# Values of eleven token tiles computed inside the attention block instead of at the end of the projection block

## The chip, the cores and the metric

The kernel is one program on one core of a Trainium2 chip. The metric is the device time of one execution in microseconds (us). TensorE is called PE here, VectorE DVE, ScalarE ACT, GpSimd POOL, and SP is the engine that issues the DMAs.

## The reference, cut to what matters

One step of a hybrid decoder layer, for a prompt of 2048 tokens and a sample group of 8 sequences of 8 tokens (64 tokens). All in float32.

```
h = RMSNorm(x)
z = h @ W_in                      # 1024 x 4608, columns shared out to three head groups
y = x + concat[A(h)*silu(g_A), B(h)*silu(g_B), C(h)*silu(g_C)] @ W_out
A: dilated sliding-window attention, 6 heads of 64, three branches merged by their softmax denominators
B: causal convolution and RG-LRU
C: HGRN2, chunkwise gated linear recurrence, 6 heads, key width 128, value width 64
final RMSNorm
```

The change touches `z = h @ W_in` for the columns of A's values (384 columns), and the HGRN2 of the 64 sample tokens.

## The kernel before, in words

There are two blocks, one behind the other, with a barrier between them in which every queue is drained.

**The projection block** (`front`) normalises the input in 17 token tiles (16 of 128 tokens, and one of the 64 sample tokens, tile 16). Each tile is turned on PE and kept as a high and a low part, `f_ht0` and `f_ht1`, of [128, 8, 2112]: eight contraction steps by all tokens. Every product with a weight is done as three matmuls (`mm3`, lines 49 to 51: high by high, high by low, low by high). Where the weights are stationary, the moving operand is a stretch of 384, 448 or 512 tokens; where a token tile is stationary, the moving operand is 384 weight columns. The values (`("t", 2, j)` in the order) are of the second kind: one token tile is 8 steps of 3 matmuls, then an ACT copy (line 665) and a store to the DRAM tensor `zt`. They are the last thing of the block, 17 tiles in a row. Between them stand the last steps of the prompt's HGRN2, which is cut into 30 units (6 heads by 5 token groups) of about 12 "slots" each; `parts()` puts the next slot into the order. Before, one slot stands behind each value tile.

**The attention block** (`attend_project`) is ordered by a list that `attend_schedule` writes. All engines walk the same list, each takes its own part of an entry, and all queues are in order. The entries that matter here:

- `s`, n: quarter n%4 of head n//4's keys (parts 0, 1) or queries (parts 2, 3). A load of 2 x 256 KB from `zf`, an ACT copy to the high part (line 1914), a DVE subtraction for the low part (2104 keys, 2108 queries), and for queries another ACT copy (1918).
- `u`, n: one of 32 units of scores of a head: 2 matmuls on PE (2353, 2354) into one of three banks, mask and minimum on DVE (2118), the exponential on ACT (1966).
- `w`, h: DVE gathers head h's statistics (2030) once its 32 units are done; `x` and `z` exchange them between partitions.
- `t`, `o`, `f`: probabilities are turned by a diagonal matrix that POOL writes (1865, PE 2412), copied on ACT or DVE (1533, 1535), multiplied with the values (2433), stored. They start 11 units behind the scores of their head, so the first is in head 1, behind its eleventh unit.
- `g`, c: the gates' sigmoid in four pieces on ACT (1963), each multiplied on POOL (1850).
- `ha` to `hz`: HGRN2 of the 64 sample tokens: gates and logarithms (1921 to 1937), scan (2140), decays on POOL (1832 to 1841) and ACT (1940 to 1945), pair products `hp` (2333), outputs `ho` (2378, 2380), state updates `hu` (2388 on PE, 2162 and 2165 on DVE), `hq`, `hr`, `hn` the output's norm (1957, 1844, 2174).

Before, the sample's HGRN2 and the gates of the first head pair stand among the 32 units of head 0, which has no `t` and `o` beside it.

Of the kernel before, what the change touches and what calls it, by code (L numbers as in the profile page):

```python
# [9 lines left out]
F32 = mybir.dt.float32  # L10
F32R = mybir.dt.float32r
# [62 lines left out]
def constants(nc, sem, con):  # L74
    made = sem("c_made")
    with nc.Block() as block:
        @block.gpsimd
        def _(pool):
# [5 lines left out]
            pool.wait_ge(made, BASE + 3)  # L84

# [27 lines left out]
def front_schedule():  # L113
# [124 lines left out]
def front(nc, sem, io, con, zf, zt, mab, mt):  # L238
# [7 lines left out]
    with ExitStack() as ctx:  # L246
        def sb(name, shape, dt=F32):
            return ctx.enter_context(nc.sbuf_tensor("f_" + name, shape, dt))

        ht = [sb(f"ht{p}", [P, KD, T], F32R) for p in range(2)]  # L250
        w_raw = sb("wraw", [P, 2 * KD * P])
        w_hi, w_lo = sb("whi", [P, 3072], F32R), sb("wlo", [P, 3072], F32R)
# [28 lines left out]
        sts = sb("sts", [P, 4 * NN + 1])  # L281
# [10 lines left out]
        lbl, tiny = sb("lbl", [P, 4, NH]), sts[:, 4 * NN:]  # L292
# [316 lines left out]
        def _(act):  # L609
# [195 lines left out]
        def _(dve):  # L805
# [11 lines left out]
            def low(i):  # L817
                t0, n = TTILES[i]
                for q in range(2):
                    dve.wait_ge(S["h_hi"], BASE + 2 * i + q + 1)  # L820
                    src = tps[2 * (i % 2) + q][:].rearrange("p (k t) -> p k t", t=P)
                    V.tensor_tensor(ht[1][:, 4 * q:4 * q + 4, t0:t0 + n], src[:, :, :n], ht[0][:, 4 * q:4 * q + 4, t0:t0 + n],
                                    ALU.subtract).then_inc(S["h_lo"], 1)
# [252 lines left out]
        def _(pe):  # L1076
# [24 lines left out]
            def product(s, k0, k1):  # L1101
# [13 lines left out]
            def tile_product(s):  # L1115
# [8 lines left out]
                for k in range(KD):  # L1124
                    if b == 0:
                        pe.wait_ge(S["t_split"], BASE + KD * a + k + 1)
                    mm = mm3(nc, bank[i % 3][:n, :AW], ht[0][:, k, t0:t0 + n], ht[1][:, k, t0:t0 + n],
# [201 lines left out]
ROOM, ROOM_END = 17600, 229376  # L1329


def attend_schedule():

# [12 lines left out]
    for h in range(NH):  # L1346
        for i in range(SB):
# [5 lines left out]
    order, made = [("s", 0), ("s", 1), ("ha", 0), ("s", 2), ("hb", 0)], 0  # L1353
    hgrn = {1: [("hc", 0)], 3: [("s", 3), ("hp", 0)], 5: [("hd", 0)], 8: [("hx", 0)], 10: [("hk", 0), ("he", 0), ("ht", 0)],
            11: [("hp", 1)], 12: [("hz", 0), ("hp", 2)], 13: [("ht", 1)], 14: [("hp", 3), ("ht", 2)], 16: [("ht", 3)],
            24: [("hq", 0)], 27: [("hr", 0)], 28: [("hn", 0)], 31: [("hs", 0)]}
    for h in range(NH):
        hgrn.setdefault(17 + h, []).append(("ho", h))
        hgrn.setdefault((23, 25, 26, 28, 29, 31)[h], []).insert(0, ("hu", h))
# [10 lines left out]
    for u in range(len(units)):  # L1370
        h, k = u // per, u % per
        order.append(("u", u))
        if h == 0:
            order += hgrn.get(k, [])
        if h + 1 < NH and k in (12, 16, 22):
# [7 lines left out]
        if (h, k) in ((0, 26), (1, 26), (3, 28)):  # L1383
            order.append(("g", (0, 1, 3).index(h)))
# [23 lines left out]
def attend_project(nc, sem, io, con, zf, zt, mt, mab):  # L1408
# [21 lines left out]
    with ExitStack() as ctx:  # L1430
# [6 lines left out]
        class Place:  # L1437


            end = ROOM  # L1440

            def __init__(self, words):
                self.at, self.words, self.used = Place.end, words, 0
                Place.end += 4 * words
# [1146 lines left out]
```

## Time and profile before

| | us |
|---|---|
| time, median of 3 runs | 1953.63 (1952.71 to 1958.79) |
| the profiled execution's own time | 1956.31 |
| its span in the trace | 1954.6 |
| PE busy | 1815.5 (93%) |
| DVE busy | 992.7 (51%) |
| ACT busy | 876.7 (45%) |
| POOL busy | 652.5 (33%) |

The busy time of PE is an average over stages. The page's line of 40 slices shows 9 tenths or more nearly everywhere; the slices that fall out are those from about 1150 to 1350 us, where its row of PE's granted clock falls too. Matmuls overlap in the records, so a stretch is read from the distance of the starts.

### The profile page before, as it was taken

Reading aid. Unit: us, or ns where it says so; the run is one execution under the profiler, and the core shown is the slowest. Engines: PE = TensorE matmul, PEld = TensorE weight load, DVE = VectorE, ACT = ScalarE, POOL = GpSimd, SP = SyncE. Lnnn points to the kernel's source line nnn. Section 1 sums busy time; section 2 is a strip of 40 time slices with the busy share of each in tenths; the row PEclk is TensorE's granted clock in tenths of the full one; section 3 lists DMA queues with packets and bytes.
Section 4 is the critical chain, followed back from the end, with each engine's and each line's share of the span. In section 5 each row is a group of like instructions: output and inputs, shape, how many; then the busy total and the mean of one; then the engine's idle time right before and its main releaser. Section 6 shows DMA issues by size and latency. Waiting matters only on the chain. (4 is left out here: it accounts for less than half of the span.)

```text
span 1954.6 us, 29631 instructions
## 1 busy us (share of the span) xinstructions
PE 1815.5 (93%) x10840; PEld 1583.7 (81%) x10840; DVE 992.7 (51%) x2034; ACT 876.7 (45%) x1650; POOL 652.5 (33%) x882
## 2 busy tenths in 40 slices
PE   6999988999999999999999995778989998999998
PEld 6978878898999899999989894557777886666665
DVE  4437644224666666666666523554545456454542
ACT  4438762114555655565555512655666431111110
POOL 1103212003565556556555411144333432112110
PEclk9999999999999999999999997779999999999999
DMA  6311111132021211102110115552341074665641
GB/s 201 94 43 34 38 57 48 58 112 71 24 58 27 56 29 47 36 23 60 28 56 25 36 51 118 132 104 72 103 103 33 25 226 148 184 211 170 184 144 50
DMA packets 181769, 162.12 MB, mean 83 GB/s; under 512 B 65433, under 2 KB 168890, under 8 KB 180858
## 3 DMA queue, kind: packets, MB, share of 16 engines
q1 hardware_dynamic: 181626, 160.24, 29.1%
q8 instruction: 87, 1.43, 0.3%
q14 instruction: 56, 0.46, 0.1%
HBM read 116.89 MB, written 46.55 MB: 84 GB/s over the span
## 5 line engine op out<-in xcount | busy, mean ns | idle before, releaser
L49 PE MATMUL f_bank<-f_ht,f_whi 128*128 128x384 f32 (+2 forms) x1080 | 403.5, 374 | 5.7 <-DVE f_wlo L831 5.7
L50 PE MATMUL f_bank<-f_ht,f_whi 128*128 128x384 f32 (+2 forms) x1080 | 383.1, 355 | 0.0
L51 PE MATMUL f_bank<-f_ht,f_wlo 128*128 128x384 f32 (+2 forms) x1080 | 382.9, 355 | 0.0
L780 ACT ACTIVATE f_scr<-f_scr 128x384 f32<-128x384 f32 (+1 forms) x210 | 114.5, 546 | 270.6 <-POOL f_scr L562 270.3
L49 PEld LDWEIGHTS f_bank<-f_ht,f_whi 128*128 128x128 f32 x1080 | 204.9, 190 | 19.9 <-DVE f_wlo L831 6.5
L50 PEld LDWEIGHTS f_bank<-f_ht,f_whi 128*128 128x128 f32 x1080 | 204.9, 190 | 13.4 <-issue 1.7
L51 PEld LDWEIGHTS f_bank<-f_ht,f_wlo 128*128 128x128 f32 x1080 | 204.2, 189 | 13.1
L1142 PE MATMUL f_tps<-f_scr 128*128 128x128 f32 x1536 | 204.6, 277 | 2.3 <-DVE f_scr L975 2.3
L1142 PEld LDWEIGHTS f_tps<-f_scr 128*128 128x128 f32 x1536 | 193.9, 192 | 5.1 <-DVE f_scr L975 2.5
L975 DVE TENSOR_TENSOR f_scr<-f_scr 128x192 f32<-128x192 f32 (+1 forms) x210 | 100.9, 481 | 180.1 <-ACT f_scr L780 179.9
L1865 POOL TENSOR_SCALAR a_diag<-c_ident,a_wt 128x128 f32<-128x128 f32 x192 | 119.3, 641 | 129.3 <-DVE a_wt L2187 97.6
L561 POOL TENSOR_TENSOR f_scr<-f_scr 128x192 f32<-128x192 f32 (+1 forms) x210 | 134.3, 639 | 82.8 <-PE f_tps L1142 80.5
L966 DVE COPY_PREDICATED f_scr<-f_scr,f_tps 128x384 f32<-128x384 int32 (+1 forms) x210 | 130.4, 621 | 44.7 <-PE f_tps L1142 35.9
L49 PE MATMUL f_bank<-f_whi,f_ht 128*128 128x384 f32 (+1 forms) x408 | 142.2, 349 | 3.1 <-DVE f_wlo L835 3.1
L50 PE MATMUL f_bank<-f_wlo,f_ht 128*128 128x384 f32 (+1 forms) x408 | 137.9, 338 | 0.0
L51 PE MATMUL f_bank<-f_whi,f_ht 128*128 128x384 f32 (+1 forms) x408 | 137.6, 337 | 0.0
L49 PE MATMUL a_s<-a_whi,a_mhi 128*128 128x512 f32 (+1 forms) x306 | 123.6, 404 | 4.7 <-DVE a_y L2283 4.7
L50 PE MATMUL a_s<-a_wlo,a_mhi 128*128 128x512 f32 (+1 forms) x306 | 120.3, 393 | 0.0
L587 POOL TENSOR_SCALAR f_scr<-f_scr,f_lbl 128x384 f32<-128x384 f32 (+1 forms) x30 | 46.0, 1534 | 211.3 <-ACT f_scr L747 211.3
L1884 POOL TENSOR_TENSOR a_small<-a_small,c_mhalf 128x1 f32<-128x1 f32 (+1 forms) x17 | 9.4, 551 | 280.8 <-DVE a_small L2287 280.8
L2433 PE MATMUL a_o<-a_pt,a_vf 128*64 128x128 f32 x480 | 68.1, 285 | 17.2 <-ACT a_pt L1533 16.2
L49 PEld LDWEIGHTS f_bank<-f_whi,f_ht 128*128 128x128 f32 (+1 forms) x408 | 76.5, 188 | 6.5 <-DVE f_wlo L835 4.9
(381 smaller groups left out, 3616.3 us busy)
## 6 DMA issues: line engine op xcount, KB each, us to landing
f_wraw<-in_w_in SPq DMA_DIRECT2D x27, 512.0 KB, 4.1
a_raw<-zf SPq DMA_DIRECT2D x48, 256.0 KB, 4.3
zt<-f_stage SPq DMA_DIRECT2D x48, 192.0 KB, 1.9
a_k<-in_ck SPq DMA_DIRECT2D x48, 192.0 KB, 3.8
a_v<-in_cv SPq DMA_DIRECT2D x48, 192.0 KB
f_scr<-in_xp SPq DMA_DIRECT2D x16, 512.0 KB, 4.6
a_x<-in_xp SPq DMA_DIRECT2D x16, 512.0 KB, 4.8
out_y_prompt<-a_y SPq DMA_DIRECT2D x16, 512.0 KB, 2.9
```

What stands on the lines that cost most here:

```text
L49: nc.tensor.matmul(out, w_hi, m_hi, start=start, stop=False)
L50: nc.tensor.matmul(out, w_hi, m_lo, start=False, stop=False)
L51: return nc.tensor.matmul(out, w_lo, m_hi, start=False, stop=stop)
L561: G.tensor_tensor(d[:, :, hs:], b[:, :, hs:], r, ALU.subtract)
L587: G.tensor_scalar(key[:, :n], key[:, :n], lbl[:, 1, h:h + 1], None, ALU.mult).then_inc(S["gated"], 1)
L780: A(lev[i % 3][:, :n], lev[i % 3][:, :n], ACT.Exp).then_inc(S["expd"], 1)
L966: V.copy_predicated(attn[:, :n].rearrange("p (j t) -> p j t", t=P), m.bitcast(I32).unsqueeze(1).to_broadcast([P, nt, P]), lp[x % 2][:, :n] ...
L975: V.tensor_tensor(e[:, :, hs:], e[:, :, hs:], q[:, :, hs:], ALU.mult).then_inc(S["xlev"], 1)
L1142: mm = nc.tensor.matmul(lp[x % 2][:, cols], left[:, cols], right[:, cols], start=True, stop=True)
L1865: G.tensor_scalar(diag[:, 2 * NC * (b % 2) + NC * far + m, :], con["ident"][:], wt[h % 2][:, far, c:c + 1], None, ALU.mult).then_inc(S["di ...
L1884: G.tensor_tensor(s[:, 2:3], s[:, 1:2], con["mhalf"][:rows_of(n), 0:1], ALU.pow).then_inc(Z["rstd"], 1)
L2433: mm = nc.tensor.matmul(out, val, pt[n % 4][:, c * P:(c + 1) * P], start=first and c == 0, stop=n in ends and c == len(blocks) - 1)
```

## The change

In the projection block the normed input is laid out tile by tile: `c_ht` is [128, 13, 2, 8, 128] (token tile, high or low, contraction step, token), and the last 448 tokens are in `c_htail` of [128, 2, 8, 448]. A moving operand of 384 or 512 tokens in the first thirteen tiles is now 3 or 4 pieces of 128 tokens. Only the first six value tiles (`J0 = 6`) stay, each with two slots of HGRN2 behind it instead of one. Both tensors and the split weights have fixed addresses now, so that they stay in place over the barrier, and the attention block's buffers lie over each other and over them in another way.

In the attention block eleven value tiles follow as 22 halves of 12 matmuls (`va`, `vb`), 7 before the first unit of scores and 15 among head 0's units, one behind every second unit; `vb` has an ACT copy to a stage buffer, and the next `va` entry on SP stores it. Waits `tile_out` and `probs_free` keep a buffer from being written before the tile under it has been used. Of the loads ahead of the first unit, the two parts of the gate's and query's sample columns go first, and the queries' raw quarters (`raw2`, `raw3`) only once value tile 7 is done. The load of the values for A (`load_v(0)`) comes at the end of head 0. The sample's HGRN2 is spread otherwise: its lower bound comes from the projection block, `h_qdb` is two small buffers that are cleared, its value blocks `h_vb` are made by POOL (`hv`) instead of ACT, the state updates `hu` and the first gates `g` stand among head 1's units, and the gates' sigmoids have four buffers.

```diff
+J0 = 6
+HT13, HTAIL, TW, FREE = 0, 13 * 2 * D, 13 * 2 * D + 2 * KD * 448, 13 * 2 * D + 2 * KD * 448 + 6 * D
+def normed(con, p, k, t0, n):
+    if t0 >= FG[-1][0]:
+        t0 -= FG[-1][0]
+        return con["htail"][:, p, k, t0:t0 + n]
+    j = t0 // P
+    return con["ht"][:, j, p, k, :] if n <= P else con["ht"][:, j:j + n // P, p, k, :]
...
-    for j in range(XTILES):
+    for j in range(J0):
         add(("t", 2, j))
         parts()
+        parts()
...
-                             ht[0][:, k, t0:t0 + n], ht[1][:, k, t0:t0 + n], k == 0, k == KD - 1)
+                             normed(con, 0, k, t0, n), normed(con, 1, k, t0, n), k == 0, k == KD - 1)
...
+    halves = [(h, j) for j in range(J0, XTILES) for h in ("va", "vb")]
+    for step in ("ha", "va", "vb", "s0", "hb", "va", "hp", "s1", "ht", "hc", "vb", "s2", "hd", "va", "vb", "hx", "s3", "va"):
...
+    later = {2: [("hu", 0)], 3: [("hu", 1), ("hv", 2)], 5: [("hu", 2), ("hv", 3)], 6: [("hu", 3), ("g", 0), ("hv", 4)],
+             7: [("hu", 4), ("hv", 5)], 9: [("hu", 5)], 10: [("hs", 0)]}
...
+        if h == 0 and k % 2:
+            order += hgrn.get(k // 2, [])
+            if halves:
+                order.append(halves.pop(0))
...
+            def store_v(j):
+                t0, n = TTILES[j]
+                sp.wait_ge(VS["out"], BASE + j - J0 + 1)
+                sp.dma_start(zt[t0:t0 + n, TV:TV + AW], stage[j % 2][:n, :]).then_inc(v_store[j % 2], 16)
...
+                elif kind == "vb" and n == J0 + 1:
+                    tile_out(sp, n)
+                    load_raw(2)
+                    load_raw(3)
...
-            for t, v in ((h_cut, 1.0), (h_tiny, 1.0e-37), (h_attn, 0.0), (h_qdb, 0.0)):
+            for t, v in ((h_cut, 1.0), (h_attn, 0.0), (h_qdb[0], 0.0), (h_qdb[1], 0.0)):
...
+                elif kind == "hv":
+                    if n >= 2:
+                        pool.wait_ge(H["us"], BASE + n - 1)
+                    G.tensor_tensor(h_vb[n % 2][:], h_vv[:, hv(n)].unsqueeze(1).to_broadcast([NS, NB, HD]),
+                                    h_rowm[:].unsqueeze(2).to_broadcast([NS, NB, HD]), ALU.mult).then_inc(H["vb_r"], 1)
...
+                elif kind == "vb":
+                    j, rows = n, TTILES[n][1]
+                    act.wait_ge(VS["sum"], BASE + j - J0 + 1)
+                    if j >= J0 + 2:
+                        act.wait_ge(v_store[j % 2], BASE + 16 * ((j - J0) // 2))
+                    A(stage[j % 2][:rows, :], v_bank[j % 2][:rows, 0:AW], ACT.Copy).then_inc(VS["out"], 1)
...
                 elif kind == "hu":
-                    if n == 0:
-                        pe.wait_ge(H["kd_copied"], BASE + 1)
-                        pe.wait_ge(H["vb_r"], BASE + NB)
+                    pe.wait_ge(H["vb_r"], BASE + n + 1)
+                    pe.wait_ge(H["kd_copied"], BASE + 2)
...
+                elif kind in ("va", "vb"):
+                    t0, rows = TTILES[n]
+                    if kind == "va" and n >= J0 + 2:
+                        pe.wait_ge(VS["out"], BASE + n - J0 - 1)
+                    for k in range(KD // 2) if kind == "va" else range(KD // 2, KD):
+                        cols = slice(k * AW, (k + 1) * AW)
+                        mm = mm3(nc, v_bank[n % 2][:rows, 0:AW], normed(con, 0, k, t0, rows), normed(con, 1, k, t0, rows),
+                                 con["whi"][:, cols], con["wlo"][:, cols], k == 0, k == KD - 1)
```

On PE, head 0's first units of scores before (names: `a_khi`, `a_klo` are the keys' high and low parts, `a_qst` the queries, `a_h_` the sample's HGRN2):

```order
L2357 MATMUL a_x<-c_ident,a_h_lrow 128x6
L2353 MATMUL a_s<-a_khi_14220,a_qst 128x128
L2354 MATMUL a_s<-a_klo_14222,a_qst 128x128
L2353 MATMUL a_s<-a_khi_14220,a_qst 128x128
L2354 MATMUL a_s<-a_klo_14222,a_qst 128x128
```

The same engine among head 0's units in the changed kernel, at the end of one half tile and the beginning of the next:

```order
L50 MATMUL a_o<-c_wlo,c_ht 128x384
L51 MATMUL a_o<-c_whi,c_ht 128x384
L2442 MATMUL a_s<-a_khi_13904,a_qst 128x128
L2443 MATMUL a_s<-a_klo_13906,a_qst 128x128
L2442 MATMUL a_s<-a_khi_13904,a_qst 128x128
L2443 MATMUL a_s<-a_klo_13906,a_qst 128x128
L2422 MATMUL a_t<-a_h_lev_13983 64x64 x6
L49 MATMUL a_o<-c_whi,c_ht 128x384
```

Between two pairs of units there are now twelve matmuls of the values; before, the first four units stood directly behind one another.

On PE in head 1, ahead of the first turned probabilities (`a_diag`), in the changed kernel:

```order
L2474 MATMUL a_t<-a_h_vb_13987,a_h_kdt 128x512
L2442 MATMUL a_s<-a_khi_13905,a_qn 128x256
L2443 MATMUL a_s<-a_klo_13907,a_qn 128x256
L2474 MATMUL a_t<-a_h_vb_13986,a_h_kdt 128x512
L2442 MATMUL a_s<-a_khi_13905,a_qst 128x256
```

The state updates (2474) stood among head 0's units before. On POOL the value blocks of two of them stand behind the four multiplications of the first gates:

```order
L1946 TENSOR_TENSOR a_gs_13933<-a_gs_13933,a_gsig_13955 128x512
L1946 TENSOR_TENSOR a_gs_13933<-a_gs_13933,a_gsig_13956 128x512
L1946 TENSOR_TENSOR a_gs_13933<-a_gs_13933,a_gsig_13957 128x512
L1946 TENSOR_TENSOR a_gs_13933<-a_gs_13933,a_gsig_13958 128x512
L1936 TENSOR_TENSOR a_h_vb_13986<-a_h_vv,a_h_rowm 64x512
L1936 TENSOR_TENSOR a_h_vb_13987<-a_h_vv,a_h_rowm 64x512
L1961 TENSOR_SCALAR a_diag<-c_ident,a_wt_13950 128x128 x24
```

So the fifth update waits for POOL behind the gates.

## Rows read from the trace of the kernel before

**Rows 1.** Busy us of the engines in stretches of 50 us, PE's granted clock, DMA

```profile
1150.00:1200.00 50.00, 44.18 (x262) 42.92 (x260) 2.09 (x7) 5.62 (x12) 2.13 (x6) 0.97 0.13 44
1200.00:1250.00 50.00, 21.74 (x117) 17.96 (x118) 30.77 (x88) 30.25 (x66) 13.22 (x24) 0.53 0.90 181
1250.00:1300.00 50.00, 35.58 (x192) 23.89 (x191) 25.31 (x83) 30.63 (x77) 14.02 (x19) 0.68 0.35 85
```

**Rows 2.** Timeline of ACT, copies of value tiles 5, 8, 15, 16 (start, us, idle before)

```profile
1145.72 0.49 ACT L665 ACTIVATE f_stage<-f_bank 128x384 f32<-128x384 f32 x1 [3.96 <-PE f_bank L51]
...
1160.94 0.49 ACT L665 ACTIVATE f_stage<-f_bank 128x384 f32<-128x384 f32 x1 [5.01 <-PE f_bank L51]
...
1190.06 0.49 ACT L665 ACTIVATE f_stage<-f_bank 128x384 f32<-128x384 f32 x1 [3.67 <-PE f_bank L51]
1194.22 0.48 ACT L665 ACTIVATE f_stage<-f_bank 64x384 f32<-64x384 f32 x1 [3.67 <-PE f_bank L51]
```

**Rows 3.** Timeline of DVE, the last instruction of the prompt's HGRN2

```profile
1163.60 0.36 DVE L1020 TENSOR_TENSOR f_scr<-f_scr 128x192 f32<-128x192 f32 x1
```

**Rows 4.** Timeline of POOL, start of the attention block

```profile
1198.72 0.14 POOL L1803 IOTA a_pcol<- 128x1 int32 x1 [35.55 <-POOLq L1655]
...
1200.38 2.65 POOL L1808 MEMSET a_h_qdb<- 128x3072 f32 x1
```

**Rows 5.** Timeline of DVE, the masks and the first keys' low parts

```profile
1200.66 2.52 DVE L2020 TENSOR_SCALAR a_pn<-a_pn,a_pcf 128x256 int32<-128x256 int32 x1
...
1204.38 0.43 DVE L1277 TENSOR_SCALAR a_pn<-a_pn 128x512 int32<-128x512 int32 x1
...
1210.01 2.29 DVE L2104 TENSOR_TENSOR a_klo<-a_raw,a_khi 128x1024 fp32r<-128x1024 f32 x2
```

**Rows 6.** Timeline of ACT, first query part, first exponential, a later query part, decays

```profile
1213.86 1.06 ACT L1918 ACTIVATE a_qn<-a_qst 128x1024 fp32r<-128x1024 f32 x1 [2.44 <-DVE a_qst L2108]
...
1218.57 0.40 ACT L1966 ACTIVATE a_pf<-a_pf,a_sf 128x128 f32<-128x128 f32 x1 [2.13 <-DVE a_sf L2118]
...
1225.66 1.04 ACT L1914 ACTIVATE a_qst<-a_raw 128x1024 fp32r<-128x1024 f32 x1
1228.21 1.06 ACT L1918 ACTIVATE a_qn<-a_qst 128x1024 fp32r<-128x1024 f32 x1 [1.51 <-DVE a_qst L2108]
...
1232.35 1.33 ACT L1945 ACTIVATE a_h_lev<-a_h_lev 128x384 f32<-128x384 f32 x3
```

**Rows 7.** DMA issues from 1194 to 1300 us (count, KB each, median us to landing)

```profile
a_raw<-zf SPq DMA_DIRECT2D x20, 256.0 KB, 4.4
```

**Rows 8.** Timeline of PE, a unit of scores and an output of HGRN2 (full clock)

```profile
1251.95 0.32 PE L2378 MATMUL a_x<-a_h_vv,a_h_attn 64*64 64x64 f32 x2
...
1253.28 0.39 PE L2353 MATMUL a_s<-a_khi,a_qn 128*128 128x256 f32 x1
1253.51 0.28 PE L2354 MATMUL a_s<-a_klo,a_qn 128*128 128x256 f32 x1
1253.72 0.33 PE L2378 MATMUL a_x<-a_h_vv,a_h_attn 64*64 64x64 f32 x2
```

**Rows 9.** Timeline of DVE, one state update, and the stall at the norm

```profile
1266.79 0.69 DVE L2162 TENSOR_TENSOR a_h_s<-a_h_s,a_h_gl 128x512 f32<-128x512 f32 x1
1267.52 0.69 DVE L2165 TENSOR_TENSOR a_h_s<-a_h_s,a_o 128x512 f32<-128x512 f32 x1
...
1280.28 0.55 DVE L2174 TENSOR_TENSOR a_h_oc<-a_x,a_h_small 64x384 f32<-64x384 f32 x1 [7.86 <-POOL a_h_small L1844]
```

**Rows 10.** Timeline of ACT, the first gates, and the first copy of turned probabilities

```profile
1269.68 1.28 ACT L1963 ACT_TABLE_LOAD   x1
1270.97 0.63 ACT L1963 ACTIVATE a_gsig<-a_gs 128x512 f32<-128x512 f32 x1
...
1277.63 1.28 ACT L1966 ACT_TABLE_LOAD   x1
...
1296.25 0.60 ACT L1533 ACTIVATE a_pt<-a_t 128x512 f32<-128x512 f32 x1 [0.29 <-PE a_t L2412]
```

**Rows 11.** Timeline of POOL, the first gate multiplication

```profile
1271.68 1.26 POOL L1850 TENSOR_TENSOR a_gs<-a_gs,a_gsig 128x512 f32<-128x512 f32 x1 [41.38 <-ACT a_gsig L1963]
```

**Rows 12.** Timeline of DVE, head 0's statistics

```profile
1285.18 0.29 DVE L2030 TENSOR_TENSOR a_exch<-a_sf,a_quarter 128x128 f32<-128x128 f32 x1
```

**Rows 13.** Groups by form from 1500 to 1600 us (busy us, mean ns)

```profile
L2354 PE MATMUL a_s<-a_klo,a_qn 128*128 128x256 f32 x16 | 4.3, 282 | 0.0
...
L2354 PE MATMUL a_s<-a_klo,a_qst 128*128 128x256 f32 x4 | 1.1, 279 | 0.0
```

More of the change, by code:

```diff
@@ L1328 @@
 KM = 3 * AW // P
-ROOM, ROOM_END = 17600, 229376
 def attend_schedule():
@@ L1372, in attend_schedule @@
         order.append(("u", u))
-        if h == 0:
-            order += hgrn.get(k, [])
-        if h + 1 < NH and k in (12, 16, 22):
+        if h == 0 and k % 2:
+            order += hgrn.get(k // 2, [])
+            if halves:
+                order.append(halves.pop(0))
+            if k + 1 == per:
+                assert not halves
+                order.append(("ve", 0))
+        if h == 1:
+            order += later.get(k, [])
+        if h and h + 1 < NH and k in (12, 16, 22):
             order.append(("s", 4 * (h + 1) + (12, 16, 22).index(k)))
@@ L1535, in evacuate @@
                 nc.vector.tensor_copy(pt[t % 4][:, :w], tp[t % 2][:, :w]).then_inc(S["copied_v"], 1)
-        raw += [vals0.again().tile(f"raw{p}", [P, SEQ // 2]) for p in (2,)] + [vals0.tile("raw3", [P, SEQ // 2])]
+        raw3 = Place(done0 + 2 * D, 2 * D)
+        raw += [raw3.tile(f"raw{p}", [P, SEQ // 2]) for p in (2, 3)]
+        ints_at = Place(FREE + 6144, 2048).tile("ints", [P, SEQ])
+        gsig0 = [turned.again().tile(f"gsig0{r}", [P, CLS]) if r == 0 else turned.tile(f"gsig0{r}", [P, CLS]) for r in range(NC)]
@@ L1551, in attend_project @@
[L1551 to L1553 removed]
+        stage = [early.tile(f"stage{r}", [P, AW]) for r in range(2)]
+        h_kk, h_qc, h_kd, h_bb, h_lk, h_qd, h_cut, h_sq = (early.tile("h_" + n, [P, W]) for n in ("kk", "qc", "kd", "bb", "lk", "qd", "cut", "sq"))
@@ new lines, in attend_project @@
+        h_rowm = late.tile("h_rowm", [NS, NB])
+        lev_at = late.used
+        h_lev = [late.tile(f"h_lev{l}", [P, W]) for l in LV]
+        late.used = lev_at
+        h_vb = [late.tile(f"h_vb{p}", [NS, NB, HD]) for p in range(2)]
+        h_lbl, h_tiny, h_op = con["lbl"], con["tiny"], bank_x
+        v_bank = [bank_o[:, b * 512:(b + 1) * 512] for b in range(2)]
+        VS = {x: sem("v_" + x) for x in ("sum", "out")}
+        v_store = [sem(f"v_store{r}") for r in range(2)]
+        NV = XTILES - J0
@@ L1563, in attend_project, with tile_out, probs_free, bank_h @@
         hw = lambda h: slice(h * P, (h + 1) * P)
+        def tile_out(eng, j):
+            eng.wait_ge(VS["sum"], BASE + j - J0 + 1)
+        def probs_free(eng, u):
+            h, i, far, m = units[u]
+            if h == 0:
+                j = NC * i + m
+                tile_out(eng, J0 + ((0, 0, 4, 1)[i] if far else 0 if j < 2 else 2 if j < 10 else 3))
+            elif h == 1:
+                tile_out(eng, XTILES - 1)
+        ring_h = [("P", 0), ("K", 0), ("K", 1)] + [("P", n) for n in (1, 2, 3)] + [("U", h) for h in range(NH)]
+        def bank_h(kind, n):
+            return bank_t[ring_h.index((kind, n)) % 2]
+        def bank_h_free(eng, kind, n):
+            e = ring_h.index((kind, n))
+            if e >= 2:
+                kind, n = ring_h[e - 2]
+                eng.wait_ge(H[{"P": "taken", "K": "kd_copied", "U": "s_new"}[kind]], BASE + n + 1)
         def hgrn_over(eng):
```

270 lines of the change are left out of this document (142 added, 128 removed).

## The prediction

> **What bounds the kernel now.** I read the busy shares first, then the table of stretches, then the timelines of each engine from the last value tiles to the first turned probabilities. PE is busy 93% of the span, so what is worth looking for is the place where it is not. The table of stretches [rows 1] shows it: from 1150 to 1200 us PE is busy 44 of 50 us at a granted clock of 0.97 (the level of 2.4 GHz), from 1200 to 1250 only 21.7 of 50 at 0.53 (mostly the level of 1.2 GHz), and from 1250 to 1300 35.6 at 0.68. In those 100 us no engine is full: DVE has 56 us, ACT 61. They are the start of the attention block and head 0's scores, where chains from engine to engine set the pace. Just ahead PE does nothing but the values, one tile every 4.16 us (1194.22 - 1190.06, [rows 2]), that is 24 matmuls of 0.173 us from start to start. The change takes eleven of these tiles from the full stretch into the loose one. In the following, B is the start of the attention block, POOL's first instruction at 1198.72 [rows 4].
>
> **The projection block.** From the copy of value tile 5 to that of tile 16 there are 1194.22 - 1145.72 = 48.5 us [rows 2], and 11 tiles of 4.16 are 45.8; the other 2.7 us are work of HGRN2's last slots on PE, which the change puts ahead of tile 5. So the block ends 45.8 us earlier if PE stays full: **-45.8**. The drain, store and barrier behind it stay as they are.
>
> The slots are two per tile now. Before, HGRN2 ended at 1163.96 [rows 3], behind ten slots with a tile each, while the new block would end on PE at about 1194.2 - 45.8 = 1148.4. The last unit's chain goes in turn through POOL, ACT, DVE and PE for each of its levels, and in the double slot behind tile 1 PE waits for ACT's copy of the turned decays with no tile in between, where before it had one. Lower bound 0 (PE had no gap there before, and the order is otherwise the same), upper bound 15.6, when the chain ends no earlier than before. One double slot costs two or three round trips of about 1 us that a tile hid; I take **+3**.
>
> The new layout changes how a moving operand is read: 3 or 4 pieces of 128 tokens instead of one. The nearest rows are scores at the full clock from 1500 to 1600 us [rows 13]: near keys, 256 columns in 8 pieces of 32, take 282 ns, far keys, 256 in one piece, 279. So at most 3 ns for each of the some 2,600 such matmuls, 8 us; since these have fewer pieces, I take **0**. The copies on ACT and DVE that write the layout have as many elements as before.
>
> **The attention block up to head 0's end.** Before, this takes from B to head 0's statistics at 1285.18 [rows 12], 86.5 us. Now:
>
> - PE starts tiles 6 and 7 at once. It then waits for the sample's pair product, which needs the gated key from DVE. DVE does its masks first, until B+11.3 (1210.01, [rows 5]). One of them, 256 elements, took 2.52 us beside POOL's memset of `h_qdb` (2.65 us, [rows 4]), while a mask of 512 took 0.43 [rows 5]. The memset is now two of 576 elements instead of 3072, so I count the masks 1 us shorter. Then 1.15 us for the keys' low part, 1.1 us for key and query, about 1.5 for the pair product, 2.1 for the second half of tile 7: B+16.
> - Only then are the queries' raw quarters loaded, 4.4 us to landing [rows 7]: B+20.5. Before, they had been there by B+11. The query part takes 1.04 us, the DVE subtraction, 1.06: 3.6 us from 1225.66 to 1229.27 [rows 6]: B+24. The decays with their table load (1.28 + 2.3) and the copy of tile 8 stand next on ACT, then the second query part with another 3.6 us: ACT is at the first exponential at B+31.5. Before it was there at B+19.9 (1218.57, [rows 6]). So the prelude is **11.6 us longer**; tiles 8 and half of 9 fit into it, 6.2 us.
> - Then PE has 32 units and 15 halves. A half is 12 x 0.173 = 2.08 us. A single unit of 256 columns takes 1253.72 - 1253.28 = 0.44, an output of HGRN2 1253.28 - 1251.95 = 1.33 [rows 8]. Two units in a row come to about 0.6 us at 128 or 256 columns (12 pairs), 0.8 and 1.05 at 384 and 512 (2 each): 10.9. HGRN2 adds 6 x 1.33 = 8 for outputs and about 5.4 for pair products and turns. With 0.15 for each entry into a half: 31.2 + 10.9 + 8 + 5.4 + 2.2 = 57.7, of which 4.2 have been done by B+30.4. ACT has about 34 us in the same time and DVE 30, so PE leads, and waits of the three score banks fall into the halves. 53.5 us of PE from B+30.4 is B+84; for a stretch at the lower clock at the start I add 1.5 to 3 us, for the last exponential 1.5. **Head 0's statistics at B+87**, against 86.5 before: +0.5. Bounds: B+79 (clock full, entries free) to B+97.
>
> **From head 0's end to the first turned probabilities.** Before this takes 1296.25 - 1285.18 = 11.1 us [rows 10, 12]. Now there are six state updates and the first gates in it. An update is 0.69 + 0.69 us on DVE [rows 9], 8.3 us for six; four stand ahead of the gates, of which some 4.5 us aren't covered. The gates: ACT loads a table twice, 1.28 us each, and does 4 x 0.63 [rows 10], 5.1 us; the four buffers spare it the alternation with POOL, which made it 9.2 us before (1269.68 to 1278.91). But POOL multiplies four times at 1.26 [rows 11], from 1.9 us behind the start, and the fifth update's value block stands behind these on POOL: 1.9 + 5 + 1.3 = 8.3 us until PE may go on with it, and behind that update PE has the units 40 to 42. Then the last two updates and units, about 4 us. 8.7 + 4.5 + 8.3 + 5.5 = 27 us: **+16**. Before, a stall of the same kind stood in head 0, DVE 7.86 us [rows 9]; it is in the 86.5. Lower bound +4 (all updates covered, gates as ACT alone), upper +20.
>
> The values for A are loaded at head 0's end, 2 MB; in the trace this took about 12 us, and they are needed 27 us later. Cover enough; if it were gone, the wait would be on PE's first `o`. Everything behind stands in the same order, and I count it the same.
>
> **Sum.** -45.8 + 3 + 0 + 0.5 + 16 = -26.3. The profiled execution took 1956.3 us with a span of 1954.6; this is 2.7 above the median of the runs. 1953.6 - 26.3 = 1927.3: **1927 us**.
>
> **Rivals.**
>
> - *The moved work is hidden altogether*: the stalls of updates and gates fall into time that before was lost too, the prelude's extra 11.6 us are made good as the halves keep the clock at the upper level. For it: 42.7 us of 100 were idle on PE in [rows 1] at a clock near 0.6. Against it: the gates' wait is on an in-order queue. -45.8 + 3 = 1911 us. Chance 0.2.
> - *The tail of HGRN2 sets the end of the projection block*: chain as long as before, +15.6 instead of 3: 1940 us. For it: one slot per tile was all that hid it. Against: the chain had waits of 4 to 10 us for PE's tiles in it. Chance 0.13.
> - *The clock stays at the lower level in the block.* Halves take 4.16 us instead of 2.08, 15 in the loop, +31 us, less the 3 counted: 1955 us, no change. For it: the granted clock was 0.53 and 0.68 in [rows 1]. [...] Chance 0.07. The Trainium skill ("TensorE: Matmul & The Clock Gate", the section on the second HAM failure mode, psum-queue depth-cycling) says that short idle times between groups of matmuls can make the clock go back and forth; [rows 1] agree that a PE with gaps gets less, and that would be this rival.
> - *Slower: the pieces of the moving operand cost time at each matmul.* It would be all over the projection block, from the first weights on. It decides from 26.3 us / 2,600 = 10 ns per matmul; at twice that, +52: 1979 us. For it: no row shows pieces 8 KB apart. Against: 3 ns in [rows 13] with more pieces. Chance 0.05.
>
> The Trainium skill ("GPSIMD Engine Reference", key points) says that GpSimd shares its SBUF interfaces with VectorE and that the two contend; the 2.52 us against 0.43 in [rows 5] agree. It stands here only for the 1 us of the masks.
>
> **How the numbers follow.** The forecast has 0.55, with its own range 1918 to 1937. Below 1908 it would take more than the whole of the moved tiles. 8 in 10 reach from the hidden case to the tail's: 1909 to 1943. Under 0.3% (5.9 us) a measurement of this kernel can't be told from no change: the clock's rival is that, in part. Faster 0.92, same 0.04, slower 0.04.
>
> **What the profile after would show.** Right: the attention block starts near 1156 (1198.7 - 42.8); value matmuls in the projection of the same 0.173 us; the first exponential 31 us behind B; PE busy over 40 of 50 us in head 0 at a clock above 0.9; statistics of head 0 at B+87; POOL's value block behind the gates with PE waiting some 3 us beyond ACT's table load; first turned probabilities at B+114. Wrong: PE gaps of over 5 us among the last six value tiles, half tiles of 4 us, or 10 ns more per matmul before 1100 us.

## The result and the profile after

The changed kernel takes 1934.2 us (median of 4 runs, 1931.0 to 1936.6) against 1955.8 (4 runs, 1952.7 to 1958.8). The ratio is 0.989 with a 95% interval of 0.986 to 0.992. A second set of 4 runs gave 1934.2 (1932.5 to 1934.7) and 0.989 (0.988 to 0.991). The forecast was 1927. By the medians the change is worth 21.6 us, where the sum said 26.3. The span of the profiled execution is 1930.1 us against 1954.6, -24.5; a second profile of the changed kernel, from the second set, has 1932.5. One of the eleven runs of the experiment e2 below took 2648.9 us at a mean granted clock of 0.64 and is left out of its figures.

Three marks split both spans: B (GpSimd's first instruction in the attention block), head 0's statistics (DVE's `a_exch<-a_sf`), and ACT's first copy of turned probabilities.

| us | start to B | B to statistics | statistics to first copy | first copy to end |
|---|---|---|---|---|
| before [rows 4, 10, 12] | 1198.7 | 86.5 | 11.1 | 658.4 |
| after | 1152.9 | 89.4 | 29.2 | 658.6 |
| after, second profile | 1158.2 | 86.5 | 28.9 | 658.8 |
| difference, first profile | -45.8 | +2.9 | +18.1 | +0.2 |
| forecast | -42.8 | +0.5 | +16 | 0 |

The table of stretches of after, with the columns of [rows 1]:

```profile
1150.00:1200.00 50.00, 37.65 (x200) 35.98 (x201) 19.72 (x50) 23.35 (x47) 13.01 (x28) 0.80 0.49 131
1200.00:1250.00 50.00, 47.76 (x326) 40.28 (x324) 24.12 (x87) 23.73 (x71) 4.42 (x4) 0.95 0.34 95
1250.00:1300.00 50.00, 37.36 (x209) 28.24 (x208) 24.68 (x65) 29.20 (x66) 22.32 (x31) 0.78 0.71 166
```

The stretch of head 0's scores is now full: PE 47.8 of 50 us at 0.95, where [rows 1] have 21.7 at 0.53. The loose place has moved on to 1250, head 1's start.

**The projection block.** One event ahead of the moved work dates the traces: ACT's last copy of a product with stationary weights, 8 us ahead of the copy of the first value tile. The first fence is from before; the second, from after, has the copy of the last value tile too:

```profile
1108.24 0.52 ACT L680 ACTIVATE f_stage<-f_bank 128x448 f32<-128x448 f32 x1
```

```profile
1105.22 0.52 ACT L700 ACTIVATE f_stage<-f_bank 128x448 f32<-128x448 f32 x1
...
1148.72 0.49 ACT L685 ACTIVATE f_stage<-f_bank 128x384 f32<-128x384 f32 x1 [3.45 <-PE f_bank L51]
```

So 3.0 us of the -45.8 had arisen by there, ahead of all moved work. From 250 to 300 and from 300 to 350 us the granted clock was 0.92 and 0.94 in the one execution and 0.93 and 0.97 in the other, and from 100 to 150 us 0.93 and 0.97. This differs from execution to execution: in the second profile of the changed kernel the same copy comes at 1110.49, 2.3 us later than before. From this event to B it is 90.48 us before and 47.70 after: **-42.8**, which is what the forecast had (-45.8 + 3). The second profile has 47.74. The +3 is idle time of PE among the double slots (start, us, in brackets the idle time before):

```profile
1115.39 0.43 PE L1177 MATMUL f_op<-f_scr 128*128 128x64 f32 x2 [0.82 <-DVE f_scr L986]
1124.12 0.55 PE L1247 MATMUL f_tps<-c_ident,f_scr 128*128 128x128 f32 x3 [0.28 <-ACT f_scr L804]
1125.98 0.88 PE L1256 MATMUL f_tps<-f_scr 128*128 128x64 f32 x6 [1.31 <-ACT f_scr L816]
1138.73 0.43 PE L1177 MATMUL f_op<-f_scr 128*128 128x64 f32 x2 [0.82 <-DVE f_scr L986]
```

That is 3.2 us in all, where the kernel before had one gap of 0.28. The third row is the round trip to ACT that the forecast named. From the dated event to the last value copy PE is busy 45.4 us less than before and idle 3.0 us more.

**From B to head 0's statistics.** B itself, the mask that [rows 5] had at 2.52 us, the memset beside it, and DVE's first low part, all of after:

```profile
1152.92 0.14 POOL L1890 IOTA a_pcol<- 128x1 int32 x1 [6.14 <-POOLq L1729]
...
1154.56 1.09 POOL L1895 MEMSET a_h_qdb<- 128x576 f32 x2
```

```profile
1154.86 0.93 DVE L2117 TENSOR_SCALAR a_ints<-a_ints,a_pcf 128x256 int32<-128x256 int32 x1
...
1162.63 1.16 DVE L2201 TENSOR_TENSOR a_klo<-a_raw,a_khi 128x1024 fp32r<-128x1024 f32 x1
```

The masks were 1.6 us shorter (1 was counted), the low part at B+9.7 (forecast B+10.3). Then PE's wait for the pair product, ACT's for the raw queries, and the first exponential:

```profile
1164.77 1.54 PE L2422 MATMUL a_t<-a_h_qc,a_h_kk 128*64 128x64 f32 x12 [3.90 <-DVE a_h_qc L2223]
```

```profile
1174.83 1.06 ACT L2012 ACTIVATE a_qst<-a_raw 128x1024 fp32r<-128x1024 f32 x1 [4.11 <-DMA a_raw<-zf]
...
1185.30 0.39 ACT L2062 ACTIVATE a_pf<-a_pf,a_sf 128x128 f32<-128x128 f32 x1
```

The exponential is at B+32.4 (forecast 31.5). The two parts of head 0 in the table of stretches, and the statistics:

```profile
1152.92:1185.30 32.38, 24.62 (x116) 23.59 (x117) 16.15 (x35) 17.66 (x27) 11.97 (x27) 0.76 0.62 161
1185.30:1242.34 57.04, 53.56 (x379) 49.42 (x378) 21.19 (x79) 26.86 (x80) 3.38 (x3) 0.96 0.26 77
```

```profile
1242.34 0.29 DVE L2127 TENSOR_TENSOR a_exch<-a_sf,a_quarter 128x128 f32<-128x128 f32 x1 [1.79 <-ACT a_pnb L2062]
```

PE is busy 53.6 of 57.0 us in the loop, so it leads there, as forecast. Statistics at B+89.4 (forecast 87). The second profile has the same two stretches:

```profile
1158.23:1189.96 31.73, 25.31 (x122) 24.33 (x122) 16.17 (x35) 17.46 (x27) 11.95 (x27) 0.80 0.63 164
1189.96:1244.74 54.78, 50.55 (x374) 46.47 (x373) 21.01 (x78) 26.55 (x80) 3.38 (x3) 1.00 0.28 81
```

**From there to the first copy.** The stretch before (first fence) and after (second):

```profile
1285.18:1296.25 11.07, 7.31 (x44) 6.61 (x45) 6.85 (x35) 7.33 (x26) 3.93 (x7) 0.50 0.92 197
```

```profile
1242.34:1271.55 29.21, 19.17 (x56) 9.36 (x57) 15.72 (x47) 12.63 (x32) 16.50 (x21) 0.54 0.56 121
```

PE works 11.9 us more and idles 6.3 us more (10.0 against 3.8); together 18.1. Nearly all the idle time is one row, and GpSimd's rows say why:

```profile
1244.77 2.03 PE L2474 MATMUL a_t<-a_h_vb,a_h_kdt 64*128 64x512 f32 x2
...
1263.10 2.07 PE L2474 MATMUL a_t<-a_h_vb,a_h_kdt 64*128 64x512 f32 x2 [9.26 <-POOL a_h_vb L1936]
```

```profile
1257.12 4.93 POOL L1946 TENSOR_TENSOR a_gs<-a_gs,a_gsig 128x512 f32<-128x512 f32 x4 [9.21 <-ACT a_gsig L2059]
1262.01 2.04 POOL L1936 TENSOR_TENSOR a_h_vb<-a_h_vv,a_h_rowm 64x512 f32<-64x512 f32 x2
```

```profile
1255.12 1.28 ACT L2059 ACT_TABLE_LOAD   x1
...
1271.55 0.60 ACT L1574 ACTIVATE a_pt<-a_t 128x512 f32<-128x512 f32 x1 [1.21 <-PE a_t L2511]
```

GpSimd stood 9.21 us in front of the gates' multiplications with the fifth value block behind them, and PE stood in front of that block. Each update also costs PE 2.0 us at the clock of 0.54.

### The profile page after: what moved, and what is told of

Its sections match the earlier page's. It is cut to its first block and busy times, and to the rows that moved or that the text cites. A ratio compares the mean times of both kernels' runs of the same rounds, so it can differ in the third digit from the quotient of the medians.

```text
span 1930.1 us, 29621 instructions
## 1 busy us (share of the span) xinstructions
PE 1811.6 (94%) x10839; PEld 1581.4 (82%) x10839; DVE 990.5 (51%) x2026; ACT 870.6 (45%) x1641; POOL 653.9 (34%) x888
## 5 line engine op out<-in xcount | busy, mean ns | idle before, releaser
L49 PE MATMUL f_bank<-c_ht,c_whi 128*128 128x384 f32 (+1 forms) x864 | 318.8, 369 | 5.7 <-DVE c_wlo L851 5.7
L50 PE MATMUL f_bank<-c_ht,c_whi 128*128 128x384 f32 (+1 forms) x864 | 303.5, 351 | 0.0
L51 PE MATMUL f_bank<-c_ht,c_wlo 128*128 128x384 f32 (+1 forms) x864 | 303.3, 351 | 0.0
L49 PEld LDWEIGHTS f_bank<-c_ht,c_whi 128*128 128x128 f32 x864 | 163.5, 189 | 16.1 <-DVE c_wlo L851 6.5
L50 PEld LDWEIGHTS f_bank<-c_ht,c_whi 128*128 128x128 f32 x864 | 163.4, 189 | 9.7 <-issue 1.1
L51 PEld LDWEIGHTS f_bank<-c_ht,c_wlo 128*128 128x128 f32 x864 | 163.1, 189 | 9.4
L1961 POOL TENSOR_SCALAR a_diag<-c_ident,a_wt 128x128 f32<-128x128 f32 x192 | 118.0, 635 | 120.4 <-DVE a_wt L2277 86.5
L607 POOL TENSOR_SCALAR f_scr<-f_scr,c_lbl 128x384 f32<-128x384 f32 (+1 forms) x30 | 46.0, 1534 | 211.3 <-ACT f_scr L767 211.3
L49 PE MATMUL f_bank<-c_whi,c_ht 128*128 128x384 f32 x256 | 90.8, 355 | 3.2 <-DVE c_wlo L855 3.2
L50 PE MATMUL f_bank<-c_wlo,c_ht 128*128 128x384 f32 x256 | 87.1, 340 | 0.0
L51 PE MATMUL f_bank<-c_whi,c_ht 128*128 128x384 f32 x256 | 87.0, 340 | 0.0
L2062 ACT ACTIVATE a_pf<-a_pf,a_sf 128x128 f32<-128x128 f32 (+3 forms) x96 | 53.5, 557 | 72.2 <-DVE a_sf L2216 71.9
```

The lines of the kernel that those rows point to most:

```text
L49: nc.tensor.matmul(out, w_hi, m_hi, start=start, stop=False)
L50: nc.tensor.matmul(out, w_hi, m_lo, start=False, stop=False)
L51: return nc.tensor.matmul(out, w_lo, m_hi, start=False, stop=stop)
L1961: G.tensor_scalar(diag[:, 2 * NC * (b % 2) + NC * far + m, :], con["ident"][:], wt[h % 2][:, far, c:c + 1], None, ALU.mult).then_inc(S["di ...
L2062: A(probs(n), probs(n), ACT.Exp, bias=stat(n, 0), scale=-1.0, accum_out=stat(n, 1)).then_inc(S["exped"], 1)
```

## The experiments

All times are medians; the changed kernel has 1934.2. Its eight runs spread from 1931.0 to 1936.6, so a difference of 5 us between medians is no larger than this spread, and is read together with the marks in the traces. "Distance" is that from head 0's statistics to the first copy.

**e1, GpSimd's value blocks ahead of the gates.**

```
-    6: [("hu", 3), ("g", 0), ("hv", 4)], 7: [("hu", 4), ("hv", 5)]
+    6: [("hu", 3), ("hv", 4), ("hv", 5), ("g", 0)], 7: [("hu", 4)]
```

> Edit to the changed kernel: GpSimd's last two value blocks of HGRN2 (for the updates of heads 4 and 5) are placed ahead of the first gates instead of behind and between them; nothing else. In the changed kernel PE waited 9.26 us for such a block, and the first copy of turned probabilities came 29.2 us after head 0's statistics. Theory (the forecast's reason for its +16: GpSimd's in-order queue holds PE): PE's wait in front of the fifth update falls below 3 us, the distance becomes 24 to 26 us, and the whole kernel is 3 to 5 us shorter than the changed one, 1927 to 1931 us. Rival (ACT's gates and table loads set the pace there whatever the order): the wait only moves to another row, the distance stays at 28 us or more and the time is the same. Against the kernel before: ratio 0.987 by the theory, 0.989 by the rival.

1929.2 us (1928.6 to 1931.3), ratio 0.987 (0.985 to 0.988). The wait of 9.26 is gone and one of 4.14 for the diagonals stands in its place; the distance is 1267.28 - 1242.60 = 24.7 us:

```profile
1258.15 2.07 PE L2474 MATMUL a_t<-a_h_vb,a_h_kdt 64*128 64x512 f32 x2
...
1265.09 1.65 PE L2511 MATMUL a_t<-a_diag,a_pna 128*128 128x128 f32 x6 [4.14 <-POOL a_diag L1961]
```

The theory holds: the order on GpSimd cost 4.5 us of the distance (4.3 against the second profile's 28.9).

**e2, the layout alone, on the kernel before.**

```
-        ht = [sb(f"ht{p}", [P, KD, T], F32R) for p in range(2)]
+        htm, htt = sb("htm", [P, 13, 2, KD, P], F32R), sb("htt", [P, 2, KD, 448], F32R)
```

(and every use of `ht` through `normed`.)

> Edit to the kernel before: the normed input is laid out tile by tile, as the change has it (thirteen token tiles with high part, low part and eight chunks of 128 columns each, and a tail of 448 tokens); nothing is moved. About 2,600 matmuls of the projection read it as moving or stationary operand, the wide ones now in 3 or 4 pieces of 128 columns that lie 8 KB apart. Theory (the forecast's 0): matmuls of 384 columns go on starting every 0.173 us, the ratio to the kernel before is within 0.997 to 1.003. Rival (the pieces cost time at each matmul, from 10 ns on as the forecast put it): 26 us or more, ratio 1.013 or higher.

1955.8 against 1955.5 us, ratio 1.001 (1.000 to 1.002). Groups by form from 500 to 1100 us, of before and then of this run (busy us, mean ns). 384 columns lie in three pieces in the new layout, 512 in four:

```profile
L50 PE MATMUL f_bank<-f_ht,f_whi 128*128 128x384 f32 x388 | 130.7, 337 | 0.0
L51 PE MATMUL f_bank<-f_ht,f_wlo 128*128 128x512 f32 x120 | 47.2, 393 | 0.0
```

```profile
L50 PE MATMUL f_bank<-f_htm,f_whi 128*128 128x384 f32 x388 | 130.6, 337 | 0.0
L51 PE MATMUL f_bank<-f_htm,f_wlo 128*128 128x512 f32 x120 | 47.1, 393 | 0.0
```

To the nanosecond the same. The pieces cost nothing that these rows show, and the rival of 10 ns is out.

**e3, value tile 7 directly behind tile 6.**

```
-  "ha", "va", "vb", "s0", "hb", "va", "hp", "s1", "ht", "hc", "vb", "s2", "hd", "va", "vb", "hx", "s3", "va"
+  "ha", "va", "vb", "s0", "va", "vb", "hb", "hp", "s1", "ht", "hc", "va", "s2", "hd", "vb", "hx", "s3", "va"
```

> Edit to the changed kernel: in the prelude the two halves of value tile 7 stand directly behind those of tile 6, ahead of the sample's key, pair product and first copy; the load of the queries' raw quarters waits for tile 7 and is issued that much earlier. Theory (the forecast's step: the late load makes the prelude 11.6 us longer): the load is issued 5 to 8 us earlier, the first exponential comes at 25 to 28 us from the start of the attention block instead of 32.4, head 0's statistics at 83 to 86 instead of 89.4, and the time is 3 to 6 us less than the changed kernel's. Rival (PE has the same sum of work up to head 0's end, and the clock is at its lower level in this stretch, so only idle time of PE can be won): statistics at 87.5 or later, 0 to 2 us.

1929.2 us (1927.6 to 1930.2), ratio 0.986 (0.985 to 0.988). The load of the queries' quarters is issued 11.4 us behind B instead of 17.3, and ACT no longer waits for it (B is 1157.61 here):

```profile
1174.49 1.04 ACT L2012 ACTIVATE a_qst<-a_raw 128x1024 fp32r<-128x1024 f32 x1
...
1185.27 0.38 ACT L2062 ACTIVATE a_pf<-a_pf,a_sf 128x128 f32<-128x128 f32 x1
```

First exponential B+27.7, statistics B+83.8: in the theory's windows, and the kernel is 5.0 us shorter. One reserve: in the second profile of the changed kernel, where B fell at 1158.23, the exponential came at B+31.7 and the statistics at B+86.5, not 89.4. Against this profile with nearly the same B the edit is worth 4.1 us at the exponential and 2.7 at the statistics. From B to the end it is 770.8 us, against 774.3 in that profile and 777.2 in the first.

**e4, the fifteen half tiles of head 0's loop in one piece ahead of it.**

```
-    for step in (..., "hx", "s3", "va"):
+    for step in (..., "hx", "s3", "va") + ("va",) * 15:
```

> Edit to the changed kernel: the fifteen half tiles that stand between head 0's units are placed in one piece ahead of the first unit, so that the values still are in the attention block but not among the scores; the rest keeps its order. This measures what the overlap is worth. Theory: PE has 15 x 2.08 = 31.2 us there in which no unit runs, and head 0's loop then takes what it took before without them: head 0's exponentials of the kernel before took 66.6 us with updates and gates in them, of which the 18 that the first stretch of head 1 now takes are gone; so statistics of head 0 at about 32 + 31 + 48 = 111 us from the start of the block, 22 more than the changed kernel, and about 1955 us, no gain over the kernel before. Rival (the loop is bound by PE whatever stands in it): it takes 57.7 - 31.2 = 26.5 us without the halves, the order of the halves makes no difference, statistics at 89 to 92 and 1932 to 1936 us.

1944.8 us (1942.0 to 1947.6), ratio 0.995 (0.993 to 0.996); statistics at B+99.9. Neither number was met: it is between the two. From B to the first exponential and from there to the statistics:

```profile
1155.06:1215.55 60.49, 53.67 (x285) 51.69 (x286) 15.46 (x31) 21.63 (x35) 11.97 (x27) 0.89 0.43 121
1215.55:1254.94 39.39, 27.73 (x211) 22.43 (x209) 21.57 (x82) 23.04 (x71) 3.38 (x3) 0.81 0.21 61
```

Without halves in it the loop takes 39.4 us, PE busy for 27.7 at a clock of 0.81. With them it takes 57.0, PE busy for 53.6 at 0.96. So 31.2 us of matmuls cost 17.6 among the units (15.4 against the second profile's 54.8): the interleaving hides 13.6 us (15.8). Of these the prelude gives back about 3 (60.5 against 32.4 + 31.2), which leaves the 10.5 by which the statistics come later and the kernel is longer.

**e6, the projection's last tiles in halves, a slot behind each.**

```
     for j in range(J0):
-        add(("t", 2, j))
-        parts()
-        parts()
+        add(("E", 2, j))
+        parts()
+        add(("t", 2, j))
+        parts()
```

(`E` is PE's first four of the eight chunks; `t` is the other four and everything else of the tile.)

> Edit to the changed kernel, in the projection block alone: each of the six last value tiles is issued on PE in two halves with one slot of HGRN2 behind each, instead of the whole tile and then two slots. PE had gaps of 0.82, 0.28, 1.31 and 0.82 us in these double slots, 3.2 in all, where the kernel before had 0.28. Theory (the forecast's +3 is what a round trip costs when no tile stands between two slots): the gaps fall below 1 us together, the attention block starts 2 to 3 us earlier at 1150 to 1151, and the time is that much less than the changed kernel's. Rival (the last unit's chain through POOL, ACT, DVE and PE sets the end): the gaps turn up in other places and the start stays within 0.5 us of 1152.9.

1929.2 us (1924.7 to 1931.1), ratio 0.986 (0.985 to 0.988). The four gaps are gone without others in their place. B is 1149.48, 3.4 us earlier than in the changed kernel, but this execution was already 2.6 us behind that one at the event that dates the traces (1107.83 against 1105.22):

```profile
1107.83 0.52 ACT L701 ACTIVATE f_stage<-f_bank 128x448 f32<-128x448 f32 x1
...
1145.28 0.49 ACT L686 ACTIVATE f_stage<-f_bank 128x384 f32<-128x384 f32 x1 [3.67 <-PE f_bank L51]
```

From there to the last value copy it is 37.45 us against 43.50, so the edit is worth 6.0 us, twice what the theory said; the run e8 below has 37.45 too. PE is idle for 3.8 us less (1.4 against 5.1), and for the same matmuls it is busy for 2.3 us less, at a clock of 0.95 instead of 0.92. So the term of +3 is shown as what it was said to be, round trips inside double slots and not the end of a chain, but taking them away gave back some clock as well. The kernel gained 5.0 us by the medians.

**e7, ACT's sigmoids early, GpSimd's multiplications in pairs.**

```
-    later = {2: [("hu", 0)], 3: ..., 5: [("hu", 2), ("hv", 3)], 6: [("hu", 3), ("g", 0), ("hv", 4)], 7: [("hu", 4), ("hv", 5)], ...
+    later = {2: [("gs", 0), ("hu", 0)], 3: ..., 5: [("hu", 2), ("hv", 3), ("ga", 0)],
+             6: [("hu", 3), ("hv", 4), ("gb", 0), ("hv", 5)], 7: [("hu", 4)], ...
```

> Edit to the changed kernel: the value blocks of the last two updates stand as in the run e1_value_blocks_first or at most two gate multiplications later, ACT's sigmoids of the first gates stand ahead of head 1's first update (four buffers hold them, their input landed by 1243.4 in the changed kernel's trace), and GpSimd's four multiplications stand in two pairs in the places where it waited for PE. With the value blocks first, PE's last wait was 4.14 us for the diagonals, which GpSimd made behind the multiplications, and the first copy of turned probabilities came 24.7 us after head 0's statistics. Theory (what is left of the +16 is GpSimd's queue: value blocks, multiplications, diagonals in a row): the diagonals begin 5 to 7 us earlier, PE's wait for them falls below 1 us, the copy comes 19 to 22 us after the statistics, and the kernel is 7 to 9 us shorter than the changed one. Rival (ACT's table loads and sigmoids, 4.8 us, now stand in front of head 1's first exponentials and PE then waits for score banks or updates instead): distance 24 us or more, no gain over e1_value_blocks_first.

1929.1 us (1925.2 to 1929.8), ratio 0.986 (0.985 to 0.988), distance 24.3: no gain over e1, as the rival had it. The theory's first steps held, the diagonals began 14.4 us behind the statistics, where e1 had 20.7, and PE's wait for them is 0.33; but ACT's copy of a raw quarter now stood behind the table loads, DVE waited for that, and PE for DVE's state:

```profile
1247.50 1.28 ACT L2059 ACT_TABLE_LOAD   x1
...
1253.09 1.04 ACT L2012 ACTIVATE a_qst<-a_raw 128x1024 fp32r<-128x1024 f32 x1
```

```profile
1254.16 2.39 DVE L2205 TENSOR_TENSOR a_qst<-a_raw,a_qst 64x1024 fp32r<-64x1024 f32 x1 [3.70 <-ACT a_qst L2012]
```

```profile
1258.87 2.04 PE L2474 MATMUL a_t<-a_h_vb,a_h_kdt 64*128 64x512 f32 x2 [3.97 <-DVE a_h_s L2257]
...
1265.12 1.62 PE L2511 MATMUL a_t<-a_diag,a_pna 128*128 128x128 f32 x6 [0.33 <-POOL a_diag L1961]
```

**e8, the edits of e3, e6 and e7 together.**

> The changed kernel with three edits at once: the last value tiles of the projection in halves with a slot behind each (3.4 us earlier start of the attention block when alone), value tile 7 directly behind tile 6 in the prelude (head 0's statistics 5.6 us nearer to the start of the block when alone), and the gates as in the run e7_sigmoids_early. Theory (three separate stretches, each on the path that sets the end): the gains add up, 3.4 + 5.6 + 7 to 9 = 16 to 18 us less than the changed kernel, span behind the start of the attention block 762 to 765 us against 777.2, time 1915 to 1919 us. Rival (they share one cover, so that what one saves the next waits for): 1922 to 1927 us.

**1917.6 us** (1915.7 to 1919.3), ratio 0.981 (0.979 to 0.982): 16.6 us under the changed kernel, and better than both kernels. The single edits had 5.0, 5.0 and 5.1 us, so within the spread of the runs they add up. B is 1148.80, statistics B+85.2, distance 24.2, rest 657.8. The time was in the theory's window, but by two errors that cancel: the tail is worth 6.0 us where 3.4 were counted (from the dated event to B it is 41.7 us), and behind B it takes 767.1 us, above the theory's 762 to 765, since the gates gave 5.0 instead of 7 to 9 and head 0 4.3 instead of 5.6 (1.4 against the second profile of the changed kernel).

**e9, e8 with the last query part ahead of the sigmoids; e10, e8 with the sigmoids three units later.**

```
e9:  -    2: [("gs", 0), ("hu", 0)]        +    2: [("s", 7), ("gs", 0), ("hu", 0)]     (s 7 left out at unit 4)
e10: -    2: [("gs", 0), ("hu", 0)]        +    2: [("hu", 0)]
     -    5: [("hu", 2), ...]              +    5: [("gs", 0), ("hu", 2), ...]
```

> The kernel of e8_three_together with one step moved: the low part of head 1's last query quarters (the step s 7: ACT's copy of the raw quarter, DVE's subtraction, ACT's second copy) stands ahead of the early sigmoids instead of behind them. In that kernel DVE waited 4.06 us for this copy behind ACT's table loads and sigmoids, and PE 4.31 us for DVE's state behind it. Theory (the early sigmoids gained nothing because they moved the wait from GpSimd's queue to ACT's): both waits fall below 1 us, the first copy of turned probabilities comes 20 to 22 us after head 0's statistics instead of 24.2, and the time is 2 to 4 us less than of e8_three_together, 1913.5 to 1915.5 us. Rival (behind these waits is the sum of PE's own work at its lower clock, six updates of 2.07 us and the units, or a wait of DVE for the same chain): 0 to 1 us, 1916.5 to 1918.5 us.

> The kernel of e8_three_together with the early sigmoids moved three units later, behind the last query part of head 1 and ahead of the third update; the multiplications stay in their two pairs. Theory (what counts is that no copy that DVE waits for stands behind the sigmoids): ACT is at the table load about 13 us behind head 0's statistics, the sigmoids are done 4.8 us later, GpSimd's last multiplication some 2 us behind that and the diagonals start there; PE's wait for DVE goes, one of 1 to 3 us for a value block or the diagonals comes, distance 22 to 24 us, 1916 to 1918 us. Rival (order on ACT is free there): as e9_last_part_ahead, 1913.5 to 1915.5 us.

e9: 1917.6 us (1914.9 to 1919.0), ratio 0.980 (0.978 to 0.981). e10: 1919.6 us (1918.0 to 1921.1), 0.981 (0.979 to 0.983). The kernel before had 1958.3 us in the runs beside these two and 1955.5 beside e8, and the intervals of all three ratios overlap, so differences of 2 us among e8, e9 and e10 are not shown by the times; the distances tell more. In e9 PE's wait for DVE has gone from 4.31 in e8 to 2.21 us, and yet the distance is 24.2:

```profile
1242.63 2.04 PE L2479 MATMUL a_t<-a_h_vb,a_h_kdt 64*128 64x512 f32 x2 [2.21 <-DVE a_h_s L2262]
```

```profile
1233.73:1257.90 24.17, 19.93 (x56) 9.59 (x57) 18.75 (x47) 12.41 (x32) 15.82 (x17) 0.53 0.63 145
```

PE is busy 19.9 of 24.2 us at 0.53, DVE 18.75; in e8 PE was busy 19.1 of 24.2 at 0.55. What is left is mainly PE's own work at the lower level of its clock. The rival of e9 held. In e10 neither side did: PE waited 5.89 us for a value block, more than the theory's 1 to 3, and its distance is 26.7, where the theory had 22 to 24. The order on ACT is not free.

```profile
1252.18 2.07 PE L2479 MATMUL a_t<-a_h_vb,a_h_kdt 64*128 64x512 f32 x2 [5.89 <-POOL a_h_vb L1941]
```

## Why the prediction was right

- **-45.8 for eleven tiles, +3 for the tail.** -42.8 and -42.7 in the two profiles from the dated event on, against -42.8; PE's busy time fell by 45.4 us and its idle time rose by 3.0. The double slots cost 3.2 us of PE, and e6 took them away. What the forecast did not see is that with these gaps closed the clock rises too, so that e6 gained 6.0. That B itself moved by 45.8 is luck: in the second profile of the changed kernel B was 1158.23, with a clock of 0.90 and 0.93 from 250 to 350 us. More than half of that came back: its statistics were at B+86.5, the end 2.4 us later in place of 5.3.
- **0 for the layout.** Shown by e2: 337 and 337 ns, 393 and 393.
- **+0.5 up to head 0's statistics.** +2.9 and +0.0 in the two profiles. The late raw load was the right reason for the long prelude (first exponential B+32.4 and B+31.7, forecast 31.5), shown by e3 (B+27.7 with the load 5.9 us earlier). What differs between the two profiles is the loop: 57.0 us at a clock of 0.96 against 54.8 at 1.00, where the forecast's 53.5 us of PE were counted at the full clock.
- **+16 for the updates and gates in head 1.** +18.1 and +17.9. The mechanism was right: GpSimd's in-order queue put the fifth value block behind the gates. From ACT's table load to the update it took 8.0 us, against 8.3; PE's wait was 9.26, as it stood there 1.3 us ahead of the table load. e1 took 4.5 us of the distance away. The size came out with some luck: of the four terms of 27, 8.7 stands on no row, and for the last updates and units the text says about 4 and the sum takes 5.5. One term was off by its reason: an update was priced by DVE's two instructions [rows 9], 1.4 us, while PE's own matmul for it is 2.0 us at the lower clock; the six are 12 of the 19.2 us that PE is busy there. In e1 and e9 19 to 20 of the 24 to 25 us are PE's own work, so that order alone had only some 5 us left to win.
- **0 behind the first copy.** 658.4 and 658.6 us; 657.8 to 659.5 in all the experiments.
- **The time.** 1934.2 is 6.9 us above the 1927.3 of the sum: 4.7 because the change was worth 21.6 us and not 26.3, and 2.2 because the kernel before has a median of 1955.8 by four runs and the forecast started from 1953.6. From the dated event to the end the two profiles have 21.5 and 24.4 us less than before. So the 24.5 by the first spans, close to 26.3, has 3.0 us in it that had arisen ahead of the change.

Of the rivals, *hidden altogether* would have needed head 1's start to be as short as before. *The tail* had its round trips but no chain behind them. *The clock at its lower level* was true of the prelude, in part (0.76), but the loop had 0.96: half tiles fill PE's gaps, and the clock rose as they did. The Trainium skill ("TensorE: Matmul & The Clock Gate", the section on the second HAM failure mode, psum-queue depth-cycling) speaks of gaps that make the clock go back and forth; e4 agrees from the other side, the same units without the halves having 0.81. *Slower by the pieces* fell with e2.

## What to carry to other kernels

Work of the engine that bounds one stage, moved into a stage where that engine idles, gains its full time where it came from and pays only in part where it lands (here 31.2 us of matmuls for 17.6), if it is cut into pieces that stand among the waits. One length of piece was tried, 2.08 us; how the gain depends on it is not shown. What it wins where it came from is only half of the account: of the 42.8 us won here, 21 were paid back behind in the one profile and 18 in the other, 18 of them for the updates and gates that had to make room. What it pushes out must be priced on every engine that takes part, the matrix engine at its lower clock included, and followed through each in-order queue it joins: a short instruction behind another engine's long chain costs the wait of the whole chain. Taking a wait off one queue by moving its cause to another engine gains only if nothing that is waited for stands behind it there either.

## What the runs showed of the hardware

- An execution that reached B 5.3 us later, with a lower clock between 250 and 500 us (0.90, 0.93 and 0.97 in three of the five stretches of 50 us, against 0.93, 0.97 and 1.00) ended only 2.4 us later. It is the same kernel in both, so the loss and the giving back are both in code that did not differ.
- Where PE's gaps were closed its granted clock was higher: 0.95 instead of 0.92 in the last value tiles (e6, the same matmuls, PE busy 36.1 us instead of 38.4), and 0.96 and 1.00 in head 0's loop with the half tiles against 0.81 without them (e4).
- DVE's mask of 256 integers took 0.93 us beside a GpSimd memset of 576 elements and 2.52 beside one of 3072 [rows 4, 5]. The Trainium skill ("GPSIMD Engine Reference", key points) names the shared interfaces; that what DVE loses depends on the length of GpSimd's instruction these two rows suggest, and no run isolated it.
- DVE's subtraction of a query quarter, 64x1024, took 1.22 us in the prelude, where GpSimd did nothing beside it, and 2.39 in e7, where GpSimd multiplied the gates beside it (rows of e7). No run isolated this either.
